# One core, a hybrid decoder layer: gate/up products begin with block b, and the border to the down projection is reordered

## What is computed

```python
h = rmsnorm(x, norm_ffn_g)
gate, new_ffn = causal_dwconv(h @ w_gate, ffn_prev, conv_ffn_w, conv_ffn_b)
x = x + (jax.nn.silu(gate) * (h @ w_up)) @ w_down
```

## Time and profile before

| | before |
|---|---|
| median of 3 runs | 2348.78 us (2340.26 to 2353.99) |
| the profiled execution | 2352.12 us, its span 2350.4 us |
| busy, share of the span: PE | 2276.6 us, 97% |
| DVE | 1688.3 us, 72% |
| ACT | 971.4 us, 41% |
| POOL | 555.5 us, 24% |
| L2108 to L2110 (gate/up products) | 6720 matmuls of 295 to 298 ns mean |
| L2167 to L2169 (down products) | 3696 matmuls of 296 to 300 ns mean |

### The profile page before, as it was taken

One profiled execution on the slowest core, in us unless ns is written; L12 is line 12 of the kernel. 1 busy time (PEld: TensorE's weight loads), 2 busy tenths in 40 slices (PEclk: granted clock), 3 DMA queues, 4 the chain that ended last, 5 costly groups with the idle time before them and its releaser, 6 DMA issues. The chain is left out here.

```text
span 2350.4 us, 43938 instructions
## 1 busy us (share of the span) xinstructions
PE 2276.6 (97%) x16978; PEld 2259.5 (96%) x16978; DVE 1688.3 (72%) x2281; ACT 971.4 (41%) x1469; POOL 555.5 (24%) x641
## 2 busy tenths in 40 slices
PE   7999999999999899999999999999998899999995
PEld 7999999999999899999999999999997899999995
DVE  6357744446322768787888888888886799888896
ACT  6224321223111444454444444444443454444454
POOL 2310000000222001111011111111113267656685
PEclk9999999999999999999999999999999999999998
DMA  7322233223433243534444344443435566765522
GB/s 245 98 81 60 73 86 90 75 86 112 155 105 101 73 137 115 163 116 149 129 140 155 113 158 129 135 147 127 152 123 210 175 218 223 235 204 191 175 86 99
DMA packets 368936, 320.09 MB, mean 136 GB/s; under 512 B 8648, under 2 KB 348739, under 8 KB 363072
## 3 DMA queue, kind: packets, MB, share of 16 engines
q1 hardware_dynamic: 346320, 203.98, 29.6%
q0 software_dynamic: 22512, 114.69, 13.0%
HBM read 258.32 MB, written 60.31 MB: 136 GB/s over the span
## 5 line engine op out<-in xcount | busy, mean ns | idle before, releaser
L1827 PE MATMUL ps<-h_hi,w_hi 128*128 128x288 f32 x1792 | 532.7, 297 | 2.2 <-issue 2.0
L1829 PE MATMUL ps<-h_hi,w_lo 128*128 128x288 f32 x1792 | 529.1, 295 | 0.0
L1828 PE MATMUL ps<-h_lo,w_hi 128*128 128x288 f32 x1792 | 528.9, 295 | 0.0
L2167 PE MATMUL ps<-form,dw_hi 128*128 128x288 f32 x1232 | 369.6, 300 | 23.6 <-DVE dw_lo L1715 21.0
L2168 PE MATMUL ps<-form,dw_hi 128*128 128x288 f32 x1232 | 365.0, 296 | 0.0
L2169 PE MATMUL ps<-form,dw_lo 128*128 128x288 f32 x1232 | 364.3, 296 | 0.0
L1827 PEld LDWEIGHTS ps<-h_hi,w_hi 128*128 128x128 f32 x1792 | 337.3, 188 | 3.5 <-issue 2.7
L1828 PEld LDWEIGHTS ps<-h_lo,w_hi 128*128 128x128 f32 x1792 | 337.2, 188 | 0.0
L1829 PEld LDWEIGHTS ps<-h_hi,w_lo 128*128 128x128 f32 x1792 | 337.1, 188 | 0.0
L1223 DVE TENSOR_TENSOR w_lo<-raw,w_hi 128x1024 fp32r<-128x1024 f32 x128 | 162.8, 1301 | 205.9 <-ACT w_hi L785 205.8
L1715 DVE TENSOR_TENSOR dw_lo<-down,dw_hi 128x512 fp32r<-128x512 f32 (+1 forms) x282 | 258.3, 928 | 51.9 <-ACT dw_hi L799 48.0
(11 more groups left out here) (289 smaller groups left out, 5195.3 us busy)
## 6 DMA issues: line engine op xcount, KB each, us to landing
raw<-in_w_gate_dram SPq DMA_DIRECT2D x88, 512.0 KB, 4.5
raw<-in_w_in_dram SPq DMA_DIRECT2D x80, 512.0 KB, 4.1
down<-in_w_down_dram SPq DMA_DIRECT2D x32, 1024.0 KB, 5.5
form<-act_scratch POOLq DMA_DIRECT2D x28, 1152.0 KB, 7.2
act_scratch<-stage POOLq DMA_DIRECT2D x46, 576.0 KB, 4.6
raw_c<-in_w_up_dram SPq DMA_DIRECT2D x40, 512.0 KB, 3.8
raw_d<-in_w_up_dram SPq DMA_DIRECT2D x40, 512.0 KB, 5.3
raw<-in_w_out_dram SPq DMA_DIRECT2D x32, 512.0 KB, 4.0
```

Source lines behind the costliest of these rows:

```text
L1827: te.matmul(out, whi, xhi, start=start, stop=False)
L1828: te.matmul(out, whi, xlo, start=False, stop=False)
L1829: return te.matmul(out, wlo, xhi, start=False, stop=stop)
L2167: te.matmul(out, dw_hi[:, m % 4, j, :], act_f[:, j, 0, :], start=start and j == 0, stop=False, skip_group_check=True)
```

## The change

- The seven products of a quad come in another order: b, a, c+d, c+d-a, b-(c+d-a), d, a-c. `quad_form`, `b_form`, `form_hi` and PE's `quad` follow; the banks stay with their forms. DVE's list behind the gate row becomes: convolution, `form_lo` 0 (b), `sum1`, `form_lo` 1 (a), `form_lo` 2, `sum2`, `sum4`; and `sum3` moves from behind `form_lo` 3 to behind `form_lo` 4 and, where they come, `act_lo` and `act_t4`. `sum3` is now the last of the four, and SP still waits for the last before it sends for c.
- The places of the first four form slots are exchanged to fit the new order.
- SP issues the weights of visit 0 when `sum4` and `form_lo` 3 of the last quad are done.
- POOL loads forms 0 and 1, then waits until the weights of visit 0 have landed, then loads forms 2 to 6.
- `sums13(0)` moves from POOL to DVE, between the last gate row and its convolution. `sums13(1)` on POOL waits for it.
- `down_lo(3)` moves ahead of the multiplication with the gate.
- The transposed rows move from visit 0 to visit 2 (PE, ACT), their transfers out from visit 1 to visit 4, the clearing of `facc` from visit 2 to 5. Forms 9, 10 and 11 are loaded in visits 3, 4 and 5, one in each. The last stores go to visits 1, 3 and 5.

```diff
-        slots = [sb(f"form{n}", ...) for n in (0, 1, 2, 3, 9, 10, 8, 7, 6, 4, 5, 11)]
+        slots = [sb(f"form{n}", ...) for n in (2, 3, 0, 1, 9, 10, 8, 7, 6, 4, 5, 11)]
...
-            return (raw[:, 0], raw_e[:, :, :], raw[:, 1], raw_e[:, :, :], raw[:, 1], raw_d[:, :, :], raw[:, 0])[t]
+            return (raw[:, 1], raw[:, 0], raw_e[:, :, :], raw_e[:, :, :], raw[:, 1], raw_d[:, :, :], raw[:, 0])[t]
...
                 if v == 0:
                     sp.wait_ge(stage_b_out, 16 * (PAIRS - 2))
-                    sp.wait_ge(lo_ready, N_LAST + 5)
-                else:
-                    sp.wait_ge(lo_ready, D0 + NQ * (v - 1))
+                    sp.wait_ge(sum_done, 4 * (FT - STD) - 1)
+                sp.wait_ge(lo_ready, N_LAST + 4 if v == 0 else D0 if v == 1 else D0 + NQ * (v - 1))
...
                 if v == 1:
                     pool.wait_ge(piece_done, D0)
+                    pool.wait_ge(s13_ready, 2)
...
-            for k, n in ((0, 1), (1, 1), (4, 2), (6, 2), (2, 3), (3, 3), (5, 4)):
+            for k, n in ((0, 1), (1, 1), (2, 2), (3, 2), (4, 3), (5, 4), (6, 3)):
+                if k == 2:
+                    pool.wait_ge(down_landed[0], 16)
                 load_form(k, piece_done, N_LAST + n)
             store_act(PAIRS - 1, 0)
-            sums13(0)
...
-                if v == 2:
-                    for k in (9, 10):
-                        load_form(k, lo_ready, D0 + 2 * NQ)
-                    load_form(11, piece_done, N_LAST + 4)
-                if v in (2, 4, 6):
-                    store_act(PAIRS - 1, v // 2)
+                elif 3 <= v <= 5:
+                    load_form(v + 6, lo_ready, D0 + 2 * NQ)
+                if v in (1, 3, 5):
+                    store_act(PAIRS - 1, (v + 1) // 2)
...
-                act.wait_ge(piece_done, n + 1)
+                act.wait_ge(piece_done, n + 2)
                 act.wait_ge(z_ready, q + HEADS)
                 a.activation(snap[:, :], ps[:, b, 0:HALF], ACT.Copy).then_inc(s1_done, 1)
...
-                act.wait_ge(piece_done, n + 2)
+                act.wait_ge(piece_done, n + 3)
...
-                if not last:
-                    sum1(*nxt)
+                if last:
+                    dve.wait_ge(down_landed[0], 16)
+                    v.tensor_tensor(down_sum(0), down_form(0, 6), down_form(0, 5), ALU.add).then_inc(s13_ready, 1)
+                    v.tensor_tensor(down_form(0, 6), down_form(0, 0), down_form(0, 6), ALU.subtract).then_inc(s13_ready, 1)
                 gate_conv(q)
...
                     form_lo(*nxt, 0)
+                    sum1(*nxt)
                     form_lo(*nxt, 1)
+                    form_lo(*nxt, 2)
                     sum2(*nxt)
-                    form_lo(*nxt, 2)
                     sum4(*nxt)
...
             c21(FT - 1, 4)
+            down_lo(3)
             times_gate(FT - 1, PAIRS - 1, 1)
             act_t32(PAIRS - 1)
-            down_lo(3)
...
-                product(i, u, 0, b, True, False)
+                product(i, u, 0, b + 2, True, True)
+                product(i, u, 1, b, True, False)
                 if first and u == 0:
                     pe.wait_ge(t_lo, 2)
-                product(i, u, 1, b + 1, True, False)
-                product(i, u, 2, b + 2, True, True)
+                product(i, u, 2, b + 1, True, False)
...
-                if vi == 0:
+                if vi == 2:
+                    pe.wait_ge(bank_read, 8)
                     states_t()
```

More of the change, by code:

```diff
@@ L174, in build_layer @@
         SLOT = JM * 2 * HALF * 4
-        slots = [sb(f"form{n}", [P, JM, 2, HALF], F32R, at=h_at + n * SLOT) for n in (0, 1, 2, 3, 9, 10, 8, 7, 6, 4, 5, 11)]
+        slots = [sb(f"form{n}", [P, JM, 2, HALF], F32R, at=h_at + n * SLOT) for n in (2, 3, 0, 1, 9, 10, 8, 7, 6, 4, 5, 11)]
         down0 = sb("down0", [P, JM, 2, 2, P], at=raw_at)
@@ L740, in _ @@
                     sums13(v + 1)
+                if v == 4:
+                    pool.wait_ge(rows_staged, 1)
+                    g.dma_start(new_ffn_prompt[0, 0].rearrange("r (t c) -> (r t) c", c=P), ffn_stage[0:2 * FT, 0, :]).then_inc(rows_out, 16)
+                    rows = new_ffn_sample[0].rearrange("b k (t c) -> (b k t) c", c=P)
+                    g.dma_start(rows[0:5 * P, :].rearrange("(n p) c -> p n c", p=P), ffn_stage[:, 1:6, :]).then_inc(rows_out, 16)
+                    g.dma_start(rows[5 * P:2 * NB * FT, :], ffn_stage[0:2 * NB * FT - 5 * P, 6, :]).then_inc(rows_out, 16)
+                    g.dma_start(new_mix_prompt[0, 0].rearrange("r (t c) -> (r t) c", c=P), mix_stage[0:16, 0, :]).then_inc(rows_out, 16)
+                    g.dma_start(new_mix_sample[0].rearrange("b k (t c) -> (b k t) c", c=P), mix_stage[:, 1, :]).then_inc(rows_out, 16)
+                if v == 5:
+                    pool.wait_ge(rows_out, 5 * 16)
+                    g.memset(facc[:, :], 0.0).then_inc(facc_done, 1)
                 if v >= VISITS:
@@ L1034, in form_hi @@
                 act.wait_ge(piece_done, n - 3)
[L1035 to L1038, removed]
+                if t < 2:
+                    act.wait_ge(raw_landed[1 - t], a_landed(i, u))
                 elif t == 5:
@@ L1041, in form_hi @@
                 else:
-                    act.wait_ge(sum_done, sums(i, u, {1: 1, 3: 2, 4: 3, 6: 4}[t]))
+                    act.wait_ge(sum_done, sums(i, u, {2: 1, 3: 2, 4: 3, 6: 4}[t]))
                 a.activation(w_hi[:, c], quad_form(t), ACT.Copy).then_inc(hi_ready, 1)
@@ L1188, in _ @@
                 bank_snap(v, 2, 3, bank_a, u2_snap)
-                if v == 0:
+                if v == 2:
                     rows_stage()
-                elif v in (2, 4, 6):
-                    act_hi(PAIRS - 1, v // 2)
+                if v in (1, 3, 5):
+                    act_hi(PAIRS - 1, (v + 1) // 2)
                 more = v + 1 < VISITS * len(CHUNKS)
@@ L1575, in sum2 @@
             def sum2(i, u):
-                dve.wait_ge(lo_ready, first_piece(i, u) + 2)
+                dve.wait_ge(lo_ready, first_piece(i, u) + 3)
                 v.tensor_tensor(raw_e[:, :, :], raw_e[:, :, :], raw[:, 0], ALU.subtract).then_inc(sum_done, 1)
             def sum3(i, u):
-                dve.wait_ge(sum_done, sums(i, u, 2))
+                dve.wait_ge(sum_done, sums(i, u, 3))
                 v.tensor_tensor(raw[:, 0], raw[:, 0], raw_c[:, :, :], ALU.subtract).then_inc(sum_done, 1)
             def sum4(i, u):
-                dve.wait_ge(lo_ready, first_piece(i, u) + 3)
+                dve.wait_ge(sum_done, sums(i, u, 2))
                 v.tensor_tensor(raw[:, 1], raw[:, 1], raw_e[:, :, :], ALU.subtract).then_inc(sum_done, 1)
@@ L1621, in _ @@
                     form_lo(1, 0, 2)
+                    sum2(1, 0)
                 act_lo(q // 2, q % 2)
@@ L1669, in quad @@
                 form_lo(i, u, 3)
-                sum3(i, u)
                 if prev:
@@ L1680, in quad @@
                     act_t4(j)
+                sum3(i, u)
                 form_lo(i, u, 5)
-                dve.wait_ge(piece_done, n + 3)
+                dve.wait_ge(piece_done, n + 2)
                 dve.wait_ge(s1_done, q - (STD - 1))
@@ L1802, in _ @@
                     down_s4(vi + 1)
-                if vi in (2, 4, 6):
-                    act_lo(PAIRS - 1, vi // 2)
-                    if vi == 2:
+                if vi in (1, 3, 5):
+                    act_lo(PAIRS - 1, (vi + 1) // 2)
+                    if vi == 1:
                         act_t4(PAIRS - 1)
@@ L2091, in b_form @@
             def b_form(t, part, j):
[L2093 to L2096, removed]
+                if t in (0, 1, 4):
+                    return hq[:, {0: 1, 1: 0, 4: 3}[t], part, j, :]
+                if t in (2, 3):
+                    return tq[:, t - 2, part, j, :]
                 if t == 6:
```

16 lines of the change are left out of this document (2 added, 14 removed).

## The result

| | before | after |
|---|---|---|
| median | 2350.85 us (4 runs, 2340.26 to 2353.99) | 2374.79 us (4 runs, 2369.67 to 2376.28) |
| ratio after to before, 95% interval | | 1.0106 (1.0070 to 1.0142) |
| the profiled execution, its span | 2352.12 us, 2350.4 us | 2375.37 us, 2373.7 us |

What follows compares the result with a forecast made beforehand. PE, busy for 97% of the span, was taken as the bound. Gains of 11.0 us (quads) and 24.0 (border), less 0.7, 0.8 and 1.5, gave 32.0 off 2352.1: 2320 us, range 2315 to 2327, chance 0.68.

Steps and rivals of the forecast that it cites:

- (1) of the quads: Quads: sum3 ends at T+11.9 instead of T+7.7 (T: last quad's start), a landing by T+22; no loss taken.
- signs of being wrong: Named in advance: a wait for form 6 over 3 us, low parts of a late, or DVE without idle time in a quad.
- (b): Rival, quads: they keep their waits, since late a or b sets a new edge; 11 us not won, 2331; chance 0.08.
- (d): Rival, quads: DVE becomes the bound, all 40 grow by 1.1 us, 44 us in all; 2375; chance 0.05.
- The lost cover: Quads: sum1 no longer hides ACT's first tap; DVE idles about 1.06 us there, against 3.7 us idle per quad.
- the snapshots: Quads: ACT's two snapshots wait 3.2 us longer, still 2 us before the product that overwrites their banks.
- the first quads: Start of the quads: b is loaded last in the first quad, landing some 4 us before it begins.
- The margin of before: Last quad before the change: a's low part is ready at 1772.4, the quad begins at 1773.0; 0.6 us.
- The border, weights: First down product: visit 0's weights, issued 3.7 us earlier, land 7 us before PE wants them; the 8.03 us wait goes.
- The border, forms: Visit 0: held-back forms 2 to 6 land later, form 6 0 to 1.3 us late; 0.7 us loss taken.
- The border, DVE: Visit 0: down_lo(3) moves ahead, its 2.30 us wait goes; DVE operations meeting POOL's sums cost 0 to 2, taken 0.8.
- Later visits: Visits 1 to 7: DVE low parts meeting POOL's sums after stores cost 0 to 6 us, 1.5 taken.

Runs made afterwards that it cites:

- e1: The kernel after the change, with sum3 put back behind form_lo 3; 2321.46 us, 0.9881 of before.
- e11: The kernel before, with only SP's issue of visit 0's weights moved earlier, behind sum4 and form_lo 3; 2337.20 us, 0.9944 of before.
- e7: The kernel after with sum3 back behind form_lo 3, and without POOL's wait for visit 0's weights between forms 1 and 2; 2321.30 us, 0.9875 of before.

## Why the prediction was wrong

**The step that failed** is (1) of the quads, the late `sum3`, which was priced at nothing. It ran the list of the last quad forward from T, once, and took "a between T + 19.5 and T + 22" for its landing, a margin. Measured from 1736.91, a was issued at T + 16.1 and landed at T + 24.8, b at T + 19.3. Two things were wrong in it. First the landing: SP's mean rate over a span was used for the bunch, and the 5.2 us of one load for its share; four in a row took 4.3, 5.4, 7.1 and 8.7. Second the open chain: "d and a stay" holds only for a quad in which DVE is not already late. A late a makes `form_lo` 1 late, and through DVE's gapless 13.5 us the issue of the next a. The text had the terms of this loop, 5.2 to 7.7 us for the load, 1.2 for ACT, the operations of DVE's list, and never added them round to compare them with 22.4. One of the signs of being wrong that it named came true: the low part of form 1 (a) was late. Sized at +11.0 us, the term was -36.8.

**The rivals.** (b) named the place, "a ... sets a new edge", and gave it 11 us not won; a loop longer than PE's pitch (the time of a quad without a wait) has no such floor and takes its excess in every pair: 47.16 - 44.73 = 2.4 us, 20 times. (d) came to 2375, the measured number, by chance, since its mechanism is another: the 0.95 us of idle time in front of the convolution is there as forecast, and e1, which has it too, has no wait in a quad. That DVE had idle time enough was right as a sum (39.7 of 200 us idle in after) and beside the point: it idled while it waited for the load in its own loop.

**The other steps of the quads.** That the waits of before would go was right in e1, which lies at 2321.5 against a forecast of 2320. The forecast's sum is in effect that of e1, since it gave the late `sum3` no price; its parts came out near there too (quads -11.8 us, visits 0 to 7 -20.1). The margin of before, read as 0.6 us, is 0.5 by the rows (1771.26 + 1.23 against 1773.0). The lost cover, the snapshots and the first quads cost nothing, as said.

**The border, weights.** Right. Issued at 1818.33, 14.7 us ahead of the first down product, they landed after 9.1 us (8.8 forecast); the 8.03 us went, and the granted clock was 1.00 from the first down product on. The price of the early issue, e11, and of the hold-back, e7, show that the first did it.

**The border, forms.** Form 6 was late by 1.93 us where 0.7 was taken and 1.3 was the upper end: its 2.2 us of excess is the term that was too small. Forms 2 to 6 landed 2.1 us apart, as taken, but for the last, which came 3.6 us behind form 5; SP had sent for the weights of visit 2 at 1839.11, while form 6 was on its way (that these slowed it is not tested).

**The border, DVE.** In visit 0 `down_lo(3)` now comes in time: the wait of 2.30 us is gone. No product waited for a low part there, so the meeting with POOL cost 0 instead of 0.8.

**Later visits.** 7.4 us of excess, of which the transposes are 1.2, so 6.2 where 1.5 was taken. The cause was named, POOL held by a store, and dismissed with "POOL's sums wait for weights there"; that is so in e1 and not in after. The visits up to 8 were to take 71.3 us and took 76.7.

The sum closes: 2320.1 + 47.8 (quads) + 5.4 (visits 0 to 7) + 2.1 (ahead of the quads and behind visit 8) = 2375.4, the profiled 2375.37.

## What to carry to other kernels

When a load is issued behind work that itself needs the load before it, add the loop up once round, from the issue through landing, high part and list to the next issue, and compare it with the bound engine's pitch; a loop longer than that costs its excess every time, however much its engines idle. Price a load at the time it takes in the company it will have, not alone and not at a mean rate: the same four took 3.8 to 5.6 us spread over 7.5 us and up to 8.7 when they left together. Where a stage can hand slack on from one turn to the next, count two turns, and look at its first turns in the trace: a start that drifts by a microsecond per turn, with no wait yet, is the loop already.

## What the runs showed of the hardware

SP's own issue of a load took 0.37 us in e1 throughout the quad shown; in after it took 1.34 and 1.44 us for the third and fourth load of one bunch and 2.04 for the fourth of the next. That earlier loads are on their way is not enough for this: in e1 a was sent for 1.5 us behind d, with d on its way, in 0.37 us. It came in bunches whose first three issues began 0.6 to 0.7 us apart. In the quads of after the queues moved 139 GB/s on the mean, the same as the 138 of before: it was the order in time and not the amount over the stage that made loads late.
